# Token sums inside the projection loop, a unit's last addition ahead of the second scaling, and the turns of the probabilities in two banks

## What is computed

```python
h = rms_norm(x, w['norm_mix_g'])
z = h @ w['w_in']                      # q, k, v, u, ga, gp
q = rope(rms_norm(q, w['q_norm_g']), pos)
k = rope(rms_norm(k, w['k_norm_g']), pos)
attn = sink_window_attention(qb, k_band, v_band, q_pos, k_pos, w['attn_sinks'])
pooled = multiscale_pool(ext, first, S)
merged = sigmoid(ga) * (attn @ w['w_attn_branch']) + sigmoid(gp) * (pooled @ w['w_pool_branch'])
x = x + merged @ w['w_out']
x = x + hier_moe(rms_norm(x, w['norm_ffn_g']), ...)
```

## Time and profile before

| | us |
|---|---|
| three runs | 1050.23, 1054.63, 1055.84 (median 1054.63) |
| the profiled execution, its own time | 1054.29 |
| its span in the trace | 1052.5 |
| TensorE busy | 910.9 (87%) |
| VectorE busy | 360.5 (34%) |
| ScalarE busy | 194.0 (18%) |
| GpSimd busy | 199.1 (19%) |
| data moved by DMA | 258.88 MB |

### The profile page before, as it was taken

The page is one execution under the profiler, slowest core; times in us unless marked ns, Lnnn a source line. Parts: engine busy times, 40 slices in busy tenths (PEclk is TensorE's granted clock), DMA queues, the critical chain, the costliest instruction groups (busy, mean ns, idle before and its releaser), DMA issues.

```text
span 1052.5 us, 11085 instructions
## 1 busy us (share of the span) xinstructions
PE 910.9 (87%) x4299; PEld 510.2 (48%) x4299; DVE 360.5 (34%) x719; ACT 194.0 (18%) x490; POOL 199.1 (19%) x169
## 2 busy tenths in 40 slices
PE   6998998888989999999769998776987887777884
PEld 5444676666668888745543343232323233232331
DVE  4688597877342224412334111011111111011110
ACT  3432333233523100011201111010000001000010
POOL 0140143223023333200011121111101011111111
PEclk9999999999999999999858999999889899999998
DMA  9523121111112227195539999999999999999992
GB/s 316 189 80 120 40 70 59 40 42 43 77 41 80 80 81 264 47 387 212 226 118 370 387 396 399 402 403 396 405 399 402 396 404 401 405 401 396 406 402 55
DMA packets 34089, 258.88 MB, mean 246 GB/s; under 512 B 8872, under 2 KB 12200, under 8 KB 18792
## 3 DMA queue, kind: packets, MB, share of 16 engines
q1 hardware_dynamic: 28000, 245.43, 58.9%
q0 software_dynamic: 6048, 12.89, 4.6%
HBM read 252.96 MB, written 14.58 MB: 254 GB/s over the span
## 4 chain that ended last, share of the span: by engine, by line
PE 55%; DMA 28%; DVE 9%; issue 3%; ACT 2%; SPq 1%; POOL 0%; POOLq 0%; DVEq 0%; ACTq 0%
DMA arena<-in_w_gu 22%; PE ps L1604 20%; PE ps L1834 12%; PE ps L1853 6%; PE ps L1543 5%; PE ps L1752 5%; DMA arena<-in_w_ed 4%; DVE win_sums L1198 2%; DMA arena<-in_x 2%; PE ps L1824 1%; PE ps L1620 1%; PE ps L1659 1%; DVE arena L1201 1%; DVE a_stat L1224 1%; PE ps L1771 1%
## 5 line engine op out<-in xcount | busy, mean ns | idle before, releaser
L1604 PE MATMUL ps<-arena 128*128 128x272 f32 x1120 | 271.2, 399 | 18.5 <-DVE arena L1174 5.5
L1834 PE MATMUL ps<-arena 128*64 128x512 f32 x512 | 238.5, 616 | 23.0 <-DMA arena<-in_w_gu 22.8
L1604 PEld LDWEIGHTS ps<-arena 128*128 128x128 f32 x1120 | 211.0, 192 | 70.9 <-issue 11.5
L1835 PE MATMUL ps<-arena 128*64 128x512 f32 x512 | 238.6, 616 | 0.0
L1853 PE MATMUL ps<-arena 128*64 128x512 f32 x512 | 136.2, 680 | 56.1 <-issue 45.6
L703 ACT ACTIVATE arena<-ps 128x272 f32<-128x272 f32 (+5 forms) x169 | 76.3, 456 | 409.0 <-PE ps L1604 183.6
L1834 PEld LDWEIGHTS ps<-arena 128*64 128x64 f32 x512 | 68.1, 141 | 164.4 <-issue 128.8
L1405 DVE SCALAR_TENSOR_TENSOR arena<-ps,list_w,arena 64x512 f32<-64x512 f32 x32 | 23.8, 743 | 294.7 <-ACT arena L923 294.7
L665 POOL DMA_INDIRECT out_y<-arena,list_i x32 | 46.1, 1441 | 410.5 <-PE ps L1824 355.2
L1853 PEld LDWEIGHTS ps<-arena 128*64 128x64 f32 x512 | 44.4, 155 | 145.2 <-issue 144.5
L1543 PE MATMUL ps<-arena 128*128 128x512 f32 (+1 forms) x192 | 73.6, 539 | 8.4 <-DMA arena<-in_w_kv 7.1
(11 more groups left out here) (209 smaller groups left out, 737.7 us busy)
## 6 DMA issues: line engine op xcount, KB each, us to landing
arena<-in_w_gu SPq DMA_DIRECT2D x64, 2048.0 KB, 45.1
arena<-in_w_ed SPq DMA_DIRECT2D x32, 2048.0 KB, 43.4
arena<-in_w_pair SPq DMA_DIRECT2D x20, 1024.0 KB, 4.8
arena<-in_x SPq DMA_DIRECT2D x8, 512.0 KB, 7.7
arena<-in_w_q SPq DMA_DIRECT2D x2, 2048.0 KB, 16.1
arena<-in_w_out SPq DMA_DIRECT2D x2, 2048.0 KB, 13.4
arena<-in_x_T SPq DMA_DIRECT2D x4, 512.0 KB, 8.8
out_y<-arena SPq DMA_DIRECT2D x4, 512.0 KB, 7.5
```

The lines of the kernel that those rows point to most:

```text
L1604: ins = mm(out, w[:, k, :], tokens[:, k, :], start=k == 0 and q in "127", stop=k == 3, skip_group_check=q not in "127")
L1834: mm(ps[0:C, 2 + s, :], xT[s][:, j, :], w[:, jj, 0, :], start=j == 0, stop=j == JX - 1)
L1835: ins = mm(ps[64:64 + C, 2 + s, :], xT[s][:, j, :], w[:, jj, 1, :], start=j == 0, stop=j == JX - 1)
```

## The change

The four token sums of the first units leave the place behind the projection loop: two of them come at tile n = 12 and two at n = 13, each pair behind the row sums of the tile. So that they can be written before the rotation is over, the rotation tables and four other small areas move to other places in the arena. The turns with odd numbers go to bank 0, the first of the scores' banks, instead of bank 4; a turn then waits for the copy of the turn two before it, an odd turn also for the first addition of the next group's maxima (which empties banks 0 and 1), and the scores wait for the copies of earlier odd turns. In VectorE's stream of an iteration the second scaling comes behind the unit's last addition C21 instead of ahead of the window sums.

```diff
-        rot = area(4352, 4, NT, HD)
-        g_qk = area(5632, 2, HD)
-        x_sq = area(5760, D)
-        ones_f = area(6784, P)
-        r_diag = area(6912, T)
+        rot = area(11968, 4, NT, HD)
+        g_qk = area(13248, 2, HD)
+        x_sq = area(13376, D)
+        ones_f = area(14400, P)
+        r_diag = area(14528, T)
@@ take_probsT
-            copy(probsT[k % 4], ps[:, 4, :]).then_inc(pT_taken[k % 2], 1)
+            copy(probsT[k % 4], ps[:, 4 - 4 * (k % 2), :]).then_inc(pT_taken[k % 2], 1)
@@ sum_tokens
             def sum_tokens(b, at):
 
+                first_sums(b)
+                last_sums(b, at)
+
+            def first_sums(b):
+
                 tt(b["t1"], b["12"], b["11"], ALU.subtract).then_inc(tsum_ready, 1)
                 tt(b["t3"], b["22"], b["12"], ALU.subtract).then_inc(tsum_ready, 1)
-                dve.wait_ge(tsum_ready, at + 1)
+
+            def last_sums(b, at):
+
+                dve.wait_ge(tsum_ready, at + 2)
                 tt(b["t2"], b["22"], b["t1"], ALU.subtract).then_inc(tsum_ready, 1)
                 dve.wait_ge(tsum_ready, at + 3)
                 tt(b["t4"], b["21"], b["t2"], ALU.subtract).then_inc(tsum_ready, 1)
@@ the projection loop, VectorE
                 if NT + 2 <= n < 2 * NT + 2:
                     scale_hT(n - NT - 2)
+                if n == 2 * NT + 2:
+                    dve.wait_ge(hT_scaled, NT)
+                    first_sums(h_parts)
+                if n == 2 * NT + 3:
+                    last_sums(h_parts, 0)
@@ behind the loop
-            dve.wait_ge(hT_scaled, NT)
-            sum_tokens(h_parts, 0)
@@ an iteration, VectorE
                 if n is not None:
                     take_c22(n)
-                if i + 1 < N_GROUP and halves[i + 1] == 2:
-                    normalise(i + 1, 1)
                 for m in POOL_BLOCKS.get(i, ()):
                     pool_block(m)
                 if n is not None:
                     take_c21(n)
+                if i + 1 < N_GROUP and halves[i + 1] == 2:
+                    normalise(i + 1, 1)
@@ scores, TensorE
                 above(pe, s_taken, first_half[i])
+                if i > 1:
+                    pe.wait_ge(pT_taken[1], first_turn[i - 1] // 2)
@@ probsT_turn, TensorE
-                above(pe, pT_taken[(k - 1) % 2], (k - 1) // 2 + 1)
+                above(pe, pT_taken[k % 2], k // 2)
+                if k % 2 == 1 and i + 1 < N_GROUP:
+                    pe.wait_ge(s_taken, first_half[i + 1] + 1)
-                    ins = transpose(ps[:, 4, j * P:(j + 1) * P], rows, ident)
+                    ins = transpose(ps[:, 4 - 4 * (k % 2), j * P:(j + 1) * P], rows, ident)
```

## The result

The changed kernel takes 1045.25 us (median of five runs, 1044.32 to 1048.20); the kernel before took 1053.12 us in the same rounds (1050.23 to 1055.84). The ratio is 0.9933, 95% interval 0.9905 to 0.9961: 7.1 us less by the ratio (4 to 10 us by the interval). The forecast was 5.7 us and 1048.6 us, with a range of 1044.3 to 1053.3. The profiled execution of the changed kernel took 1046.36 us, its span is 1044.5 us.

A forecast was written before the change was run, and what follows sets the result against it. TensorE, 87% busy, was taken as the bound; its progress starts the final expert-weight stream, so front savings move everything. 4.9 + 1.85 + 2.4 - 2.15 - 1.3 = 5.7 us off 1054.29 gave 1048.6 us, range 1044.3 to 1053.3.

The forecast's parts named there:

- token sums: Unit 0, end of projection: product "6" starts 3.1 us earlier and keeps full clock, saving 1.8 more; 4.9 us won.
- turns, iterations 2 and 3: Odd turns no longer wait for VectorE's copy of the even turn: 1.1 us and 0.75 us, together 1.85 us won.
- turns, iterations 5 and 6: Same stalls of 1.38 us before odd turns as in iteration 2; 1.2 us won in each, 2.4 us together.
- late maximum of group 8: Iteration 6: scaling now runs beside GpSimd's weight sums, ends near 265.9 us, and delays the next maximum by 2.15 us.
- clock at the third mix: TensorE's hole before the third mix grows from 0.90 to 3.0 us, so the clock falls; 1.3 us lost.
- new limit: Iteration 2: mixing waits for ScalarE's copy of turn 7 until 169.0 instead of 170.1, so only 1.1 us is won.
- The analogy with 119.94: Scaling in iteration 6 drawn out as at 119.94 us beside GpSimd's second sum, where four multiplications took 2.77 us.
- The signs: Product "6" near 101 us takes 2.1; no copy waits before odd turns; iteration 6 scaling over 3; third mix waits over 2.5.
- B: Rival: scaling behind the addition costs nothing, slipping between GpSimd's sums; 9.1 us gained, 1045.2 us; chance 0.18.
- C: Rival: clock falls at 101 us all the same; 1050.4 us, or 1052 if ScalarE swallows iterations 5 and 6; chance 0.22.
- D: Rival: slower, scaling meets GpSimd's sums in iterations 0, 1, 4, 5 too, costing 8.6 us; 1057.2 us; chance 0.07.
- E: Rival: the front's gain does not reach the end, as the expert stream's length varies by more; 1054 us; chance 0.07.

The follow-up runs named there:

- experiment 7: Changed kernel plus five matmuls with unread output in the hole before the third mix; 1045.31 us against 1054.38 for the kernel before, ratio 0.9910.
- experiment 9: The changed kernel itself, unaltered, run again on another chip; 1045.58 us against 1054.12 for the kernel before, ratio 0.9924.
- experiment 2: Against the kernel before, only odd turns to bank 0 with their waits, and moved tables; sums and scaling as before; 1045.88 us against 1052.88, ratio 0.9935.
- experiment 4: Changed kernel with the second scaling behind the unit's last addition only in iterations 0, 1, 4, 5; 1040.92 us against 1052.88 for the kernel before, ratio 0.9890.
- experiment 5: Changed kernel with the second scaling ahead of the window sums in all iterations, as before; 1044.14 us against 1054.38 for the kernel before, ratio 0.9900.
- experiment 6: Changed kernel with GpSimd's weight sums of unit 9 held until iteration 6's second scaling is done; 1041.31 us against 1054.38 for the kernel before, ratio 0.9879.
- experiment 3: Against the kernel before, only the second scaling behind the unit's last addition, and moved tables; sums and banks as before; 1062.41 us against 1052.88, ratio 1.0083.
- experiment 8: Experiment 4 plus matmuls with unread output in four other holes (units 0, 5 and 9); 1039.35 us against 1054.38 for the kernel before, ratio 0.9863.
- experiment 11: Experiment 8 again, unaltered, on another chip; 1039.99 us against 1054.12 for the kernel before, ratio 0.9857.

## Why the prediction was right, and where its steps were not

The measured 7.1 us lie within the range, 1.4 us above the forecast. By the marks of the profiled execution:

| step | forecast | from the stages | why |
|---|---|---|---|
| token sums | 4.9 | 5.4, less 1.4 of clock | P-S0, S0-S1 |
| turns, iterations 2 and 3 | 1.85 | 2.8 | S3-S4, S4-S5 |
| turns, iterations 5 and 6 | 2.4 | 3.5 | S6-S7, S7-S8 |
| late maximum of group 8 | -2.15 | -2.2 | S8-M with the hole filled |
| clock at the third mix | -1.3 | -1.4, or 0 | S8-M, experiments 7 and 9 |
| clock behind the hole before unit 9's product "6" | - | -1.4, or 0 | M-W |
| sum | 5.7 | 5.4, 9.5 where the clock holds | |

That the profile's 5.4 us are so near to the 5.7 of the forecast is luck in part. The turns were put 2.0 us too low, the token sums 0.5, and two falls of the clock of 1.4 us each were not foreseen; the errors nearly cancel. What the clock does differs between executions of the same program (347.5 and 343.6 us from P to W), and the measured 7.1 us lie between the two.

**Token sums.** The slack in the loop was as counted: all of it but the last 0.37 us, which the forecast had not spent, vanished, and the last transposition came behind a hole of 1.89 us, for which I had 2.2. Counted from P, product "6" starts 3.5 us earlier (forecast 3.1) and takes 1.9 us less (forecast 1.8). Product "6" kept its clock as forecast. What I did not see is the next hole, 1.93 us before product "5", 5.6 us behind the first. In the kernel before, with the same hole of 1.93 us there, the granted clock had been at 0.50 up to 107 us and was at 1.00 from 108 us on, ahead of the hole; now the two holes stand near each other at full clock, and in most profiles the clock falls in the second. That their nearness does it is not shown, as no run has one of them alone filled. The step "I take the clock as kept, 4.9 us in all" held for the product named and failed for the one after the next.

**The turns.** The step that failed is the path of iterations 2, 5 and 6, the "new limit": "ScalarE's copy of turn 7 comes after its exponentials ... Mixing starts at 169.0 instead of 170.1". The mixing of values takes its first half from the two even turns (loop over kb outside the loop over v) and needs ScalarE's last copy only for its second half. ScalarE's row in the changed kernel, copies of turn 7 and of U4 together, stands beside the mixing at 166.19 above:

```profile
166.60 0.85 ACT L703 ACTIVATE arena<-ps 128x512 f32<-128x512 f32 x2
```

The mixing began 0.4 us ahead of that copy and lost only 0.16 us on the way (2.10 instead of 1.94). So iteration 2 won 2.0 us and not 1.1, and iterations 5 and 6 won 2.0 and 1.5 and not 1.2 each. I had taken a wait for the whole operation where it is a wait for its second half. Experiment 2 shows that the banks alone bring 1.6 us in each of the three; the order adds 0.4 and 0.5 in iterations 2 and 5 and takes 0.1 in iteration 6 (experiments 4 and 5).

**The order.** Forecast as worth nothing beyond the banks in iterations 0, 1, 4 and 5: it brings 0.8 us (experiments 4 and 5). Forecast as costing 3.45 us in iteration 6: 3.58 in the profile of after. The analogy with 119.94 held to 0.1 us (2.23 us late, forecast 2.15), and experiment 6 shows its cause. Its four multiplications took between 0.34 and 1.42 us each. The prediction's step from the rule of the locked ports to a scaling that "could not end before GpSimd's last sum does" is more than the rule gives, as a lock held for one instruction leaves room between two sums; here the scaling did end 0.7 us behind the last one.

**The signs.** Product "6", the copies of the turns, the scaling and the third mix did as said. That the stage behind 310 us keeps its 136 us did not hold in this profile: it lost 1.4 us to the clock. It held in experiment 9 (M-W 168.36).

**The rivals.** B (the late scaling costs nothing) is refuted by 3.10 us against 1.14. C (the clock falls at 101 us all the same) did not happen in any profile with the sums moved; its cost came at product "5" instead, at 1.4 us. D (the contention doubles in the iterations with window sums) is refuted by S1-S3, 34.80 against 34.84, which fits the prediction's reading that running the scaling last only changes which operation of VectorE loses the time. Its direction was right for the order taken alone, 8.7 us slower, but by another mechanism, holes that join. E (the front does not reach the end) is refuted by the ratios; what it rests on, a last stage that varies by 6 us, is real. With the falls of the clock it is why 7.1 us by the ratio, 7.9 by the medians and 5.4 or 9.3 between P and W can stand for one change, with the 1.7 us said above left open.

## What to carry to other kernels

Before moving an operation behind a release, ask what else runs at its new place: here 1.5 us of work became 3.8 beside another engine's sums, and that is to be read off any earlier place of the trace at which the two met. A gain in one place can join two short holes of TensorE into one that costs the clock, so count holes after the change by length and not in sum; and take a wait to the exact instruction that has it, as an operation in two halves may need the late input only for the second. When the end of a kernel varies by more than the change, compare distances between marks of one execution.

## What was not expected of the hardware

Behind holes of about 1.9 to 3.3 us the clock fell in some executions and not in others, of the same program and at the same place. Behind two holes of 1.90 and 1.93 us it fell in six of eight profiles of kernels that have both unfilled (S0-S1 is then 12.9 to 13.1 us long instead of 11.6). Behind 2.81 us it fell in nine of eleven profiles (16 matmuls in 5.62 us, 6.95 in experiment 3), not in experiments 6 and 9 (3.94). Behind 2.84 us before product "6" of unit 9 it fell in six of eleven. Behind 3.1 us before the third mix it fell in the changed kernel and not in experiment 9, the same program. Ahead of all edits it fell in five of thirteen. The length alone doesn't decide: 2.64 us (experiment 3) and 2.95 us (experiment 4, at 32.5 us) cost nothing, 2.29 us (experiment 2, at 31.4 us) did. Matmuls in the hole whose result nobody reads kept it at full speed every time, at the five filled places of experiments 7 and 8 and again at the four of experiment 11. At the third mix that says little, as one of two unfilled holes kept it too; at the other four, where it fell in most executions, eight of eight is hardly chance. What decides in an unfilled hole was not tried.

The last 600 us, in which no edit of this study changes anything, took 599.8 to 605.7 us with the same bytes moved (258.9 MB in all). Why is open.
